# Matrix memory: the next step's decays beside the numerators, step loads in three rooms; the norm of the MLP's input inside the value projection

## The reference, cut to what matters

```python
def mlstm_chunk(state, q, k, v, logi, logf):
    cm, nv, m = state
    b = jnp.cumsum(logf, axis=-1)
    log_d = jnp.where(order, b[..., :, None] - b[..., None, :] + logi[..., None, :], -jnp.inf)
    log_inter = b + m[..., None]
    m_row = jnp.maximum(log_inter, jnp.max(log_d, axis=-1))
    s = jnp.einsum('bhqd,bhkd->bhqk', q, k) * jnp.exp(log_d - m_row[..., None])   # scores times decays
    a = jnp.exp(log_inter - m_row)
    num = jnp.einsum('bhqk,bhkv->bhqv', s, v) + a[..., None] * jnp.einsum('bhvk,bhqk->bhqv', cm, q)
    den = ...
    h = num / jnp.maximum(jnp.abs(den), jnp.exp(-m_row))[..., None]
    return mlstm_state_update(state, k, v, logi, logf), h
```

```python
hx = modulate(x, norm_mix_g[layer], sh1, sc1)      # rmsnorm(x, g) * (1 + scale) + shift
u, v = jnp.split(jax.nn.gelu(hx @ w_in), 2, axis=-1)   # each half 2048 wide
v = layernorm(v, ln_g, ln_b)...
```

## Time and profile before

| | us |
|---|---|
| median of 3 runs (lowest, highest) | 4540.08 (4534.22, 4540.29) |
| the profiled execution | 4536.73 |
| its span in the trace | 4535.0 |
| TensorE busy in the span | 4070.3 (90%) |
| VectorE busy | 2801.5 (62%) |
| ScalarE busy | 1056.3 (23%) |
| GpSimd busy | 660.4 (15%) |

### The profile page before, as it was taken

How to read it: one execution, slowest core, us unless ns; L and a number is a source line. 1 busy time by engine, 2 the same in 40 slices (tenths; PEclk the granted TensorE clock), 3 DMA queues, 4 the chain that set the end, 5 groups by cost and what they waited for, 6 DMA issues and landing times. The chain is left out here.

```text
span 4535.0 us, 42063 instructions
## 1 busy us (share of the span) xinstructions
PE 4070.3 (90%) x14786; PEld 1972.1 (43%) x14786; DVE 2801.5 (62%) x4383; ACT 1056.3 (23%) x2005; POOL 660.4 (15%) x497
## 2 busy tenths in 40 slices
PE   8999998997889899886849999988999994999996
PEld 3444444693444454446423333334354541333332
DVE  3555554544667417655767777755646476778775
ACT  3334452244010311273121111112210112111111
POOL 1010110200000002293102222210000000222220
PEclk9999999998999999898969999999999996999998
DMA  5122225547537221107239999962012105999995
GB/s 116 45 65 70 65 68 162 159 125 251 149 102 241 71 51 58 42 1 217 58 137 333 346 337 329 331 226 72 12 51 72 51 36 200 331 330 331 338 345 201
DMA packets 495132, 739.91 MB, mean 163 GB/s; under 512 B 131094, under 2 KB 237430, under 8 KB 494968
## 3 DMA queue, kind: packets, MB, share of 16 engines
q1 hardware_dynamic: 471752, 694.28, 44.4%
q0 software_dynamic: 10016, 36.18, 3.0%
q10 hardware_dynamic: 13200, 7.34, 0.6%
HBM read 660.65 MB, written 77.06 MB: 163 GB/s over the span
## 5 line engine op out<-in xcount | busy, mean ns | idle before, releaser
L507 PE MATMUL ps<-hT,pr_w 128*128 128x512 f32 x1344 | 590.7, 597 | 5.1 <-issue 3.8
L507 PEld LDWEIGHTS ps<-hT,pr_w 128*128 128x128 f32 x1344 | 255.2, 192 | 321.3 <-issue 318.4
L2742 PE MATMUL ps<-X,moe_hT 128*128 128x512 f32 x512 | 224.1, 596 | 0.0
L2742 PE MATMUL ps<-moe_wd,moe_hT 128*128 128x512 f32 x512 | 222.4, 592 | 0.0
L2847 DVE TENSOR_TENSOR ffn_w12g<-ffn_w12g,ffn_w11g 128x1024 f32<-128x1024 f32 x64 | 78.2, 1222 | 158.4 <-DMA ffn_w11u<-in_moe_w_up 158.4
L2742 PEld LDWEIGHTS ps<-X,moe_hT 128*128 128x128 f32 x512 | 96.6, 191 | 115.9 <-issue 115.9
L2742 PEld LDWEIGHTS ps<-moe_wd,moe_hT 128*128 128x128 f32 x512 | 96.0, 190 | 114.8 <-issue 114.8
L2354 DVE TENSOR_TENSOR X<-X,ps 128x512 f32<-128x512 f32 x192 | 118.2, 681 | 35.4 <-PE ps L2303 34.2
L2723 PE MATMUL ps<-ffn_w22g,moe_xg 128*64 128x512 f32 x256 | 122.2, 612 | 18.8 <-POOL moe_xg L2686 17.5
L2681 POOL TENSOR_TENSOR moe_xg<-moe_xT 128x256 f32<-128x256 f32 x16 | 77.4, 4839 | 387.0 <-ACT moe_xT L2803 387.0
L2077 PE MATMUL ps<-ple_w,mix 128*128 128x512 f32 x256 | 121.1, 629 | 6.0 <-DMA ple_w<-in_ple_w_gate 6.0
(11 more groups left out here) (805 smaller groups left out, 8903.4 us busy)
## 6 DMA issues: line engine op xcount, KB each, us to landing
moe_wd<-in_moe_w_down SPq DMA_DIRECT2D x32, 2048.0 KB, 16.8
X<-in_moe_w_down SPq DMA_DIRECT2D x32, 2048.0 KB, 18.4
ffn_w12g<-in_moe_w_gate SPq DMA_DIRECT2D x32, 1024.0 KB, 8.5
ffn_w12u<-in_moe_w_up SPq DMA_DIRECT2D x32, 1024.0 KB, 11.9
ffn_w21g<-in_moe_w_gate SPq DMA_DIRECT2D x32, 1024.0 KB, 12.7
ffn_w21u<-in_moe_w_up SPq DMA_DIRECT2D x32, 1024.0 KB, 14.1
ffn_w11g<-in_moe_w_gate SPq DMA_DIRECT2D x60, 512.0 KB, 10.8
ffn_w11u<-in_moe_w_up SPq DMA_DIRECT2D x60, 512.0 KB, 12.2
```

What stands on the lines that cost most here:

```text
L507: ins = eng.matmul(C.ps[r % NRING][:, :], w[:, (n // 2) % NW, k, (n % 2) * P:(n % 2 + 1) * P], HT[:, k, half * BANK:(half + 1) * BANK], st ...
L2742: ins = eng.matmul(C.ps[6 + half][:, :], hT[:, QK * h + k, :], down(q, h)[:, k, half * BANK:(half + 1) * BANK], start=(h == 1 and k == 0), ...
```

## The change

In the matrix memory: the step loads get three rooms in place of two (the first is a part of `HA` that is free by then, with its own columns); step 0 is loaded by SP in the attention stage; `og` is loaded after the load of m = 3 in place of m = 2. On VectorE the decays of step j + 1 are made after the `SD` of step j and before its denominators; ScalarE takes their exponentials at the same place of its order, after the `kw` of both groups. In the MLP: the stage "n5" is gone, and its work is written into `stage_gmlp_v`, with the products in the order 1, 3, 0, 2, 4, 5, 6 of `SEVEN`, whose first two need the first half of the tokens alone; the turns of tiles 4 to 7 stand between the four parts of the first product.

```diff
+FIRST_HALF_FIRST = tuple(SEVEN[p] for p in (1, 3, 0, 2, 4, 5, 6))
...
-def stage_gmlp_v(nc, C, A, HT, V, wt, small):
+def stage_gmlp_v(nc, C, A, S, X, HT, V, wt, small, gain, shift):
+    SEVEN = FIRST_HALF_FIRST
+    QUARTERS = ((1, 1), (0, 1), (0, 0), (1, 0))
...
+        pair = lambda t, i: C.ps[4 + 2 * (t % 2) + i]
...
+            def rows(th):
+                for t in range(th * TH, (th + 1) * TH):
+                    eng.dma_start(X[:, t, :], S.d["xacc"][t * P:(t + 1) * P, :]).then_inc(s_load[t], 16)
+            rows(0)
             for cg in range(CG):
                 for kh, c in (QUARTERS if cg == 0 else ((1, 0), (1, 1), (0, 0), (0, 1))):
...
+                    if cg == 0 and (kh, c) == QUARTERS[0]:
+                        rows(1)
...
+            for t in range(TH):
+                turn(t)
             for q, (cg, p) in enumerate(split):
                 a, b, _ = SEVEN[p]
+                if q < 2:
+                    eng.wait_ge(s_evv, TH * (q + 1))
+                    eng.wait_ge(s_eva, TH * (q + 1))
...
+                    if q == 0:
+                        turn(TH + k)
...
+            scale(0)
+            for t in range(TH):
+                scale(t + 1)
+                evac(t)
+            normed(0)
             sums(0)
+            for t in range(TH, NT):
+                if t + 1 < NT:
+                    scale(t + 1)
+                evac(t)
+                sums(1, (t - TH,))
+            normed(1)
...
-def stage_ml(nc, C, S, Cst, HX, MB, og, head_gain, first):
+def stage_ml(nc, C, S, Cst, HX, MB, og, head_gain, first, step0):
...
+        ks = [step0.k] + [[x[:, :, :] for x in two(f"k{i}", [P, GH, P])] for i in g2]
...
+        NS = len(ks)
...
             def load(m, g):
-                par, t0 = m % 2, token(g, m) * P
-                if m >= 2:
-                    eng.wait_ge(s_S[g], m - 1)
-                if m - 2 >= NG:
-                    eng.wait_ge(s_h[g], m - 1 - NG)
...
+                if m >= NS:
+                    eng.wait_ge(s_S[g], m - NS + 1)
+                if m - NS >= NG:
+                    eng.wait_ge(s_h[g], m - NS - NG + 1)
+                i = m % NS
+                load_step(eng, S, m, g, ks[i][g], vs[i][g], qs[i][g], bcs[i][g], cols[i][g], s_ld[i][g])
-            for m in range(NM):
+            for m in range(1, NM):
                 for g in g2:
                     load(m, g)
-                if m == NG:
+                if m == NS:
...
-                    if j >= 0:
-                        eng.wait_ge(s_df[g], j + 1)
+                if 0 <= j + 1 < NT:
+                    for g in g2:
+                        eng.wait_ge(s_df[g], j + 2)
                         eng.activation(f(DT[g]), f(DT[g]), ACT.Exp, scale=-1.0).then_inc(s_DT[g], 1)
...
+            def decay(j):
+                m = j + NG
+                bc, col = bcs[m % NS], cols[m % NS]
+                for g in g2:
+                    eng.wait_ge(s_ld[m % NS][g], loaded(m))
+                    if j:
+                        eng.wait_ge(s_SD[g], j)
+                    for h in range(GH):
+                        ins = eng.scalar_tensor_tensor(DT[g][:, h, :], bc[g][:, 0, h, :], col[g][:, 0, h:h + 1], far[g][:, :],
+                                                       ALU.subtract, ALU.max)
+                    ins.then_inc(s_df[g], 1)
...
                     for g in g2:
                         eng.wait_ge(s_DT[g], j + 1)
                         eng.wait_ge(s_qk[g], j + 1)
                         eng.scalar_tensor_tensor(f(SD[g]), b[g][:, :], scale, f(DT[g]), ALU.mult, ALU.mult).then_inc(s_SD[g], 1)
+                if 0 <= j + 1 < NT:
+                    decay(j + 1)
...
-def stage_attn(nc, C, A, S, MB):
+def stage_attn(nc, C, A, S, MB, step0):
...
+            for g in range(2):
+                load_step(eng, S, 0, g, step0.k[g], step0.v[g], step0.q[g], step0.bc[g], step0.cols[g], step0.s[g])
...
-        stage_norm(nc, C, "n5", X, HT, gains[:, 1, 0, 0, :], mod[:, 1, 0:KD, 0], src=S.d["xacc"])
...
-            stage_gmlp_v(nc, C, A, HT, V, UT, small[0])
+            stage_gmlp_v(nc, C, A, S, X, HT, V, UT, small[0], gains[:, 1, 0, 0, :], mod[:, 1, 0:KD, 0])
```

More of the change, by code:

```diff
@@ L2937, in stage_gmlp_v @@
         sa, sb_ = st.sb("sumA", [P, K2, BANK]), st.sb("sumB", [P, K2, BANK])
+        xn, junk = st.sb("xn", [P, 2, D]), st.sb("junk", [P, D])
+        ssq, rms, rstd = (st.sb(x, [P, NT]) for x in ("ssq", "rms", "rstd"))
+        s_load = [st.sem(f"loaded{t}") for t in range(NT)]
+        s_ssq, s_rms, s_rstd, s_xn, s_tr, s_evv, s_eva = (st.sem(x) for x in ("ssq", "rms", "rstd", "xn", "turned", "evac_v", "evac_a"))
+        pair = lambda t, i: C.ps[4 + 2 * (t % 2) + i]
         stats = st.sb("stats", [P, NT, 2 * CG, 6])
@@ L2950, in stage_gmlp_v @@
         nb = [sum(two(r, 1) for r in range(q)) for q in range(NQ + 1)]
[L2951 to L2954, removed]
+        born = [{o[:2] for r in range(p) for o in SEVEN[r][2]} for p in range(NP)]
+        puts_of = [[o for o in SEVEN[p][2] if o[:2] not in born[p]] for p in range(NP)]
+        adds_of = [[o for o in SEVEN[p][2] if o[:2] in born[p]] for p in range(NP)]
+        nput = [sum(len(puts_of[r % NP]) * TH for r in range(q)) for q in range(NQ + 1)]
+        nacc = [sum(len(adds_of[r % NP]) * TH for r in range(q)) for q in range(NQ + 1)]
+        ends = {1: (0, 1), 3: (1, 0), 5: (0, 0), 6: (1, 1)}
         final = [(cg, p) for cg in range(CG) for p in sorted(ends)]
@@ L3032, in deviations @@
                     eng.activation(sd[:, t:t + 1], ag[:, t, 1:2], ACT.Sqrt, bias=C.eps[:, 0:1]).then_inc(s_sd, 1)
+            root(0)
+            root(1)
+            for t in range(NT):
+                if t + 2 < NT:
+                    root(t + 2)
+                evac(t)
             for cg in range(CG):
-                puts(cg * NP)
-                puts(cg * NP + 1)
+                for p in range(3):
+                    puts(cg * NP + p)
                 for p in sorted(ends):
@@ L3044, in _, with scale, evac, normed @@
         def _(eng):
-            def sums(q):
+            def scale(t):
+                eng.wait_ge(s_rms, t + 1)
+                eng.reciprocal(rstd[:, t:t + 1], rms[:, t:t + 1]).then_inc(s_rstd, 1)
+                eng.wait_ge(s_rstd, t + 1)
+                if t >= 2:
+                    eng.wait_ge(s_tr, 2 * (t - 1))
+                eng.tensor_scalar(xn[:, t % 2, :], X[:, t, :], rstd[:, t:t + 1], None, ALU.mult).then_inc(s_xn, 1)
+            def evac(t):
+                eng.wait_ge(s_tr, 2 * t + 1)
+                for k in range(KD // 2):
+                    ins = eng.tensor_scalar(HT[:, k, t * P:(t + 1) * P], pair(t, 0)[:, k * P:(k + 1) * P], gain[:, k:k + 1], shift[:, k:k + 1],
+                                            ALU.mult, ALU.add)
+                ins.then_inc(s_evv, 1)
+            def normed(th):
+                eng.wait_ge(s_evv, TH * (th + 1))
+                eng.wait_ge(s_eva, TH * (th + 1))
+            def sums(q, ks=range(K2)):
                 cg, p = split[q]
@@ L3049, in sums @@
                 pb = max((r for r in range(q) if two(r, 1)), default=None)
-                for k in range(K2):
+                for k in ks:
                     if len(a) > 1:
@@ L3995, in stage_ml @@
         token = lambda g, m: m if g == 0 else (NG - 1 - m if m < NG else NG + NM - 1 - m)
-        loaded = lambda m: 16 * (4 if m < NG else 4 + 6 * ((m - NG) // 2 + 1))
+        loaded = lambda m: 16 * sum(4 if i < NG else 6 for i in range(m % NS, m + 1, NS))
         scale = float(P ** -0.5)
@@ L4029, in _ @@
         def _(eng):
[L4030 removed]
+            for v in vs:
                 for g in g2:
[L4032 removed]
+                    eng.memset(v[g][:, :, P:P + 1], 1.0).then_inc(s_one, 1)
             def decayed(j):
@@ L4470, in mixer_ab @@
         stage_ab_proj(nc, C, A, X, HA, S, gains, mod)
-        stage_attn(nc, C, A, S, MB)
+        step0 = StepRoom(nc, S, HA, [sb(f"col0{g}", [P, 3, ML_H]) for g in range(2)])
+        stage_attn(nc, C, A, S, MB, step0)
         W = A["ab_w_out_2"][0]
```

107 lines of the change are left out of this document (68 added, 39 removed).

## The result

The kernel after takes 4508.29 us (median of five runs, 4504.59 to 4517.4) against 4536.74 for the kernel before (five runs): ratio 0.9945, 95% interval 0.9934 to 0.9956. The forecast, 4520.5 on 4540.08, was 0.9957, just outside that interval. The profiled execution takes 4516.25 us with a span of 4514.3; before it was 4536.73 and 4535.0. So the two traces differ by 20.7 us, where the sum of the prediction was 19.6. The executions of one kernel spread by more than these 0.7 us, and a part of the spread lies ahead of the changed stages: in the fourteen traces of this study the matrix memory starts anywhere from 2040.3 to 2053.7 us, behind code that differs at most by the early loads of step 0.

A forecast was written before the change was run, and what follows sets the result against it. The prediction took TensorE to bound the value projection, and loads up to T(1), then VectorE's chain, the changed matrix memory. 12.9 + 6.7 = 19.6 us off the median 4540.1 gave 4520.5, range 4509 to 4534.

The forecast's parts named there:

- Value projection: MLP's value projection, bound by TensorE: its first product starts earlier, over the norm's second half; -6.7 us.
- both covers: Value projection: tiles 4 and 5 load in time, 2.6 us in hand for tile 4; later products hide their other work.
- the rest of the stage at nothing: Value projection after the second product: no cost, as products cover sums and adds; a gap per column group would cost some 3 us.
- Matrix memory: Matrix memory stage: loads bind up to T(1), then VectorE's own chain; -12.9 us.
- T(7): End of the last state update of step 7 in the matrix memory; forecast 2168.6, which is 12.9 less.
- T(0) and T(1): Ends of the last state updates of matrix memory steps 0 and 1; forecast about 2086 and 2102.
- A full step: Matrix memory from j = 2 on: VectorE's chain with `qa` amid the decays takes 11.1 us, bounds 10.0 and 12.5.
- The two reciprocals: Matrix memory, step 5: two reciprocals of roots add 0.4 us, making the step 11.5.
- the cover of the early step: Step 0's 1.58 MB hide in the attention stage; without that cover they cost 6 us of the chain of loads.
- Loads as the bound: Rival: at 186 GB/s loads set matrix memory steps of 14.1 us, its change gives nothing, 4533.5 remains; chance 0.17.
- faster steps: Rival: decays and `qa` don't meet, or loads come faster; matrix memory steps of 10.0 us, total 4515; chance 0.14.
- The slow clock: Rival: TensorE at the lower clock for nearly whole matrix memory steps, which then take 15.1 us; total 4559; chance 0.05.

The follow-up runs named there:

- the five executions: The changed matrix memory in the kernel after, its second measurement and three other changed kernels; T(7) 113.3 to 116.0 us behind the stage's first DMA.
- the wait: Against the kernel after, GpSimd waits for the decays of both groups before it scales that step's queries; one run, 4500.21 us.
- the repeat: The kernel after measured once more, nothing changed; ratio to before 0.9948 (0.9934 to 0.9962).
- the matrix memory alone: The matrix memory's change with the norm and value projection of the kernel before; ratio to before 0.9964 (0.9952 to 0.9976).
- the three with the second product by banks: Kernel after with the second product waiting per bank: alone 4514.43 us; with GpSimd's queries behind the decays 4497.22; also with `og` loaded last 4499.2.
- the pause: Kernel after with two unused VectorE scalings before the projection's last normalisation, so the u half starts later; one run, 4505.73 us.

## Why the prediction was right, step by step

**Value projection.** Predicted -6.7, measured -7.2 in its stretch. The first matmul was forecast 20 us behind the first DMA of `X` and came at 20.3; the second product 22 us behind it came at 21.2, with the gap of 1.64 for the forecast 1.7. The difference comes from the first product with its four turns: 19.6 us, where the forecast had 16.2 + 4.4 = 20.6. No later gap opened, and both covers held: the first product waits for the sum, not for a late tile. But the step "the rest of the stage at nothing" ended at the stage's border, and the price lay behind it: the u half's first matmuls stay 4 us longer at 1.2 GHz and the part behind costs 2.3 us net. I had weighed the clock inside the stages I changed, never in the next one. Of the 7.2 some 5 remain by the marks.

**Matrix memory.** Predicted -12.9 at T(7), measured -16.4, or -15.9 from the stage's first DMA (-15.6 to -18.3 over the five executions). The mechanism was right and most of the sizes were off in one direction. T(0) and T(1) came at 2086.1 and 2102.0, forecast 2086 and 2102. T(1) is right with two errors that cancel: the last load landed at 2093.2, 2.1 us sooner than the forecast 2095.3, but four decays beside two `qa` took 3.88 us, where I had 1.1 and half a `qa`. A full step was forecast at 11.1 and takes 10.5: `SD` at 2.5 for 2.6, decays with `qa` 3.23 for 3.5, and a chain of 4.95 that starts with the last decay for 5.05. Nearly half of the gap is the meeting: `qa` lies whole inside the decays and adds 1.04 of its 1.34 us, not all of it. The two reciprocals that I put into step 5 stand in step 6 and take 0.24 us there; step 6 has decays of 4.03 us and lasts 11.3, not 12.5. Steps 2 to 4 make 1.5 of the 3.5 us by which T(7) came sooner than forecast, steps 5 and 6 another 1.0 and 1.2, and step 7, 9.5 for 9.3, takes 0.2 back. Steps 2 and 7 hang on the clock, though: with 11.5 to 11.9 and 8.69 in the other executions, step 2 is longer than forecast there and step 7 shorter.

**What each part is worth.** The rooms, the early step and the gate's place give 11.8, the order of VectorE 4.1 more (3.8 to 6.5). The prediction had seen that the order holds T(1) back and that full steps grow from 10.1 to 11.1; it had not told its gain, in the last steps, from that of the rooms. For the cover of the early step I had 6 us; the run without it shows 3 to 4 at the first DMA of `X` and 3 to 6 at T(7), so that term was rather too large.

**The rivals.** Loads as the bound fell: DMA reached 253 GB/s where that rival had 186. It is real with one room less, though, as the run with two rooms shows: +32 us. In the new order faster steps than 10.4 came only where the decays and `qa` did not meet (steps 2 to 5 with the wait, step 2 with the gate's load two steps later), and then they were 9.4. The slow clock did not take hold of whole rows of steps: it is 1.00 from step 3 to step 5. But it came for single ones: step 7 of the kernel after at 0.90 takes 0.84 us more than at 1.00, and step 2 of the repeat at 0.84 about 1 us more than at 0.96. And it came in a stage where I hadn't looked.

**A rule weighed again.** The Trainium skill (SBUF — State Buffer, "Who interferes with whom") has an instruction of VectorE with two SBUF inputs kept out by one of GpSimd that reads SBUF. For `qa` the runs bear it out in the main: the decays take 3.23 us with it inside and 2.18 when it runs behind them, so 1.05 of its 1.34 us are added. For the scaling of `og` they don't: the four decays at 2093.23 ended at 2097.1, while a scaling ran from 2095.5 to 2098.4, as in the earlier trace rows.

**The sum.** -15.3, -7.2, +2.3 and -0.5 ahead of the stages make -20.7 in the traces, against -19.6: a missed loss and a gain that was sized too low almost cancel, so that the sum came this close is partly luck. The medians differ by 28.4 us, those of the repeat by 23.7. Between the two traces of the kernel after 5.3 of 6.1 us lie ahead of the changed stages; for the medians no trace shows where the difference lies.

## What to carry to other kernels

Work taken a step ahead puts its loads a step ahead too: count the rooms first, since the same order with one room less cost 32 us, where with three rooms it gained 4 to 6. When two engines meet on one path, try the one wait that parts them; here a single line on GpSimd gave 7 to 9.5 us at T(7), more than the new order did. Price a change of TensorE's work also in the stage behind it, by the granted clock of that stage's first matmuls. And before a difference of a few microseconds is put down to an edit, look how far the same stage spreads in other executions: here by up to 2.7 us.

## What the runs showed of the hardware

The clock's rise behind an idle stretch doesn't follow from the matmuls that come after it alone. With the same u half it came some 8 us behind the stage's start in six kernels (before, the matrix memory alone, the three with the second product by banks, the pause) and about 12 us behind it in eight executions of seven others, the kernel after twice among them. It came sooner when the stage started 2.5 us later. The 4 us more at 1.2 GHz cost about 2.2 us: the first matmul of the next stage comes 129.1 to 129.6 us behind the u half's first weight DMA in the former, 131.4 to 131.7 in the latter. What sets it stays open.
